# VectorE sums the halves of a value product before it takes a gate reciprocal

## The reference

```
s = einsum('bqkgd,bskd->bkgqs', qb, k) * scale ; p = softmax(s)
ob = einsum('bkgqs,bskd->bqkgd', p, v)
o  = concat(rms_norm(oa) * (1 - lam_init) * silu(ga), ob * silu(gb))
x  = x + gate * (o @ w_out)
```

## Time and profile before

| | |
|---|---|
| median of 3 runs | 1225.95 us (1225.51 to 1226.72) |
| profiled execution, its own time | 1226.55 us |
| its span, first to last instruction | 1224.7 us |
| TensorE busy | 1188.2 us, 97% |
| VectorE busy | 838.8 us, 68% |
| ScalarE busy | 587.2 us, 48% |
| GpSimd busy | 255.0 us, 21% |
| mean granted TensorE clock | 0.998 |

### The profile page before, as it was taken

The page is one execution under the profiler, slowest core; times in us unless marked ns, Lnnn a source line. Parts: engine busy times, 40 slices in busy tenths (PEclk is TensorE's granted clock), DMA queues, the critical chain, the costliest instruction groups (busy, mean ns, idle before and its releaser), DMA issues. The chain is left out here.

```text
span 1224.7 us, 16455 instructions
## 1 busy us (share of the span) xinstructions
PE 1188.2 (97%) x5915; PEld 958.7 (78%) x5915; DVE 838.8 (68%) x1266; ACT 587.2 (48%) x1240; POOL 255.0 (21%) x439
## 2 busy tenths in 40 slices
PE   5899999999999999999999999999999999999996
PEld 3455788788887888888888888888878888788885
DVE  4445488877778777767767675767757574879764
ACT  5522324546455464545646455556556655212223
POOL 1211032012030120222222322222233322210111
PEclk9999999999999999999999999999999999999999
DMA  9999242735537366363544545353544412956644
GB/s 352 370 378 378 88 113 78 206 94 173 159 104 202 94 178 167 92 170 93 140 142 121 144 119 143 105 160 90 150 148 118 130 57 76 316 166 224 190 143 176
DMA packets 169777, 200.47 MB, mean 164 GB/s; under 512 B 11760, under 2 KB 129168, under 8 KB 168928
## 3 DMA queue, kind: packets, MB, share of 16 engines
q1 hardware_dynamic: 155824, 153.65, 41.0%
q0 software_dynamic: 13424, 45.20, 11.5%
q10 hardware_dynamic: 448, 0.57, 0.1%
HBM read 166.20 MB, written 33.18 MB: 163 GB/s over the span
## 5 line engine op out<-in xcount | busy, mean ns | idle before, releaser
L806 PE MATMUL z_ps<-w_hi,xt_hi 128*128 128x512 f32 x1350 | 543.7, 403 | 2.7 <-issue 1.1
L808 PE MATMUL z_ps<-w_hi,xt_lo 128*128 128x512 f32 x1350 | 526.9, 390 | 0.0
L807 PE MATMUL z_ps<-w_lo,xt_hi 128*128 128x512 f32 x1350 | 526.5, 390 | 0.0
L1113 ACT ACTIVATE w_hi<-w_raw 128x512 fp32r<-128x512 f32 x270 | 169.3, 628 | 384.2 <-PE z_ps L808 260.9
L806 PEld LDWEIGHTS z_ps<-w_hi,xt_hi 128*128 128x128 f32 x1350 | 253.9, 188 | 72.4 <-issue 27.2
L808 PEld LDWEIGHTS z_ps<-w_hi,xt_lo 128*128 128x128 f32 x1350 | 253.4, 188 | 54.6
L1575 DVE TENSOR_TENSOR w_lo<-w_raw,w_hi 128x512 fp32r<-128x512 f32 x270 | 193.0, 718 | 149.7 <-ACT w_hi L1113 149.1
L807 PEld LDWEIGHTS z_ps<-w_lo,xt_hi 128*128 128x128 f32 x1350 | 254.3, 188 | 43.3
L2059 POOL TENSOR_TENSOR sg<-sg,zs 128x128 f32<-128x128 f32 (+1 forms) x60 | 42.8, 713 | 406.5 <-DVE sg L1645 406.3
L1676 DVE TENSOR_REDUCE small<-s_sb 128x2 f32<-128x1536 f32 (+1 forms) x60 | 87.7, 1462 | 40.1 <-ACT s_sb L1113 40.1
L1276 ACT ACTIVATE s_sb<-s_sb,small 128x768 f32<-128x768 f32 (+1 forms) x120 | 98.1, 821 | 9.7 <-DVE small L1676 9.6
(11 more groups left out here) (203 smaller groups left out, 1317.9 us busy)
## 6 DMA issues: line engine op xcount, KB each, us to landing
w_raw<-in_w_in_dram SPq DMA_DIRECT2D x188, 256.0 KB, 3.4
ada_raw<-in_w_ada_dram SPq DMA_DIRECT2D x64, 512.0 KB, 11.6
p_spill<-s_sb SPq DMA_DIRECT2D x56, 384.0 KB, 2.8
w_raw<-in_w_out_dram SPq DMA_DIRECT2D x64, 256.0 KB, 4.0
p_pair<-p_spill SPq DMA_DIRECT2D x64, 192.0 KB, 3.9
gate_raw<-in_w_ada_dram POOLq DMA_DIRECT2D x12, 1024.0 KB, 8.2
p_block<-p_spill SPq DMA_DIRECT2D x96, 96.0 KB, 2.4
w_raw<-in_w_in_dram POOLq DMA_DIRECT2D x20, 256.0 KB, 6.3
```

What stands on the lines that cost most here:

```text
L806: pe.matmul(out, hi_l, hi_r, start=start, stop=False)
L807: pe.matmul(out, hi_l, lo_r, start=False, stop=False)
L808: return pe.matmul(out, lo_l, hi_r, start=False, stop=stop)
L1113: return act.activation(out, in_, ACT.Copy, **kw)
```

## The change

In a step in which a value product and a gate reciprocal both stand, VectorE now adds the halves first. The list `early_values` holds the V entries of such a step; they are done ahead of `gate_inverse` and left out of the later loop. Such steps are 7, 9 and 11, and `o_high` has work in them while the four pairs of G heads are attended to. For D heads the same code runs and issues nothing.

```diff
--- before.py
+++ after.py
@@ -1934,14 +1934,20 @@
                         norm_reduce(it - 1)
                     if c_step == 2:
                         v_lo(it - 1)
+                    early_values = [(a, t) for kind, a, t in late if kind == "V"] if s in gate_at(it) else []
+                    for a, t in early_values:
+                        if not v_first(late):
+                            o_high(a, t)
                     if s in gate_at(it) and group_kind(it - 1) != "KV":
                         gate_inverse(it - 1, gate_at(it)[s])
+                else:
+                    early_values = []
                 for kind, a, t in late:
                     if kind == "QK":
                         qk_los(a)
                     elif kind == "S":
                         score_max(a, t)
-                    elif kind == "V" and not v_first(late):
+                    elif kind == "V" and not v_first(late) and (a, t) not in early_values:
                         o_high(a, t)
                     elif kind == "GT":
                         gated_turned(a, t)
```

## The result

The changed kernel takes 1231.39 us (median of 6 runs, 1231.01 to 1232.47) against 1226.4 for the kernel before (also the median of 6 runs): 5.0 us or 0.4% slower, ratio 1.004 with a 95% interval of 1.003 to 1.005. The prediction was 5.1 us slower and 1231.0. Its profiled execution has a span of 1229.5 us (before 1224.7), a granted TensorE clock of 0.998 as before, and the same 16455 instructions.

What follows compares the result with a forecast made beforehand. TensorE, busy 1188.2 of 1224.7 us, was taken to bound the kernel. Steps 7, 9 and 11 summed to -0.12+0.2+1.19 = +1.27 us per item, times 4 +5.1, giving a median of 1231.0 us (1229.5 to 1232.3).

Steps and rivals of the forecast that it cites:

- The bank wait goes: Step 7: TensorE's second score piece no longer waits for the sum; 0.49 of 0.75 us kept at the third piece.
- The gain is lost again before tile 1's value product: Step 8: later transposes hold the row maximum, so only 0.12 us per item of step 7's 0.49 stays.
- no contention: Rival 1: GpSimd's multiply yields to w_lo, 1227.2 us, no measurable change; chance 0.14 together with rival 4, no effect.
- The multiply meets w_lo: After each swapped reciprocal, GpSimd's gate multiply lengthens VectorE's w_lo, the weight's low part, by 0.41 us per swap.
- Step 9's cover is just used up: Step 9: a delay of 1.94 us meets 1.75 of cover before the row maximum; loss 0.2 us per item.
- Step 11 has no cover of that kind: Step 11: the same 1.94 us, without idle time before the low parts, delays tile 3's value product; loss 1.19 per item.
- the slow restart: Step 11's term for TensorE after its stall at tile 3's value product: 0.08 us per item.
- The cover of 0.83: Slack of VectorE's low parts before TensorE reaches tile 3's value product: 0.83 us.
- Nothing catches up behind it: After step 11, TensorE's later queue is late too, and ScalarE and VectorE follow it, so the loss stays.
- The full block: Rival 2: w_lo fully blocked by the multiply, or p_pair late for tile 4; 1232.7 to 1233.5 us, chance 0.14.
- The faster one: Rival 3: the whole 0.75 us per item stays and step 11's lateness misses TensorE; 1222.9 us, chance 0.05.
- The change that does nothing: Rival 4: the sum waits for ScalarE anyway; within rival 1's time of 1227.2 us, chance 0.14 together with rival 1.

Runs made afterwards that it cites:

- the single swaps: Three kernels with the swap in step 7, 9 or 11 alone, the other steps as before: 1226.09, 1227.59 and 1231.34 us against 1226.61 for the kernel before.
- the kernel with the gated row first: Kernel before, but in step 7 VectorE takes the sum and the gated row ahead of the gate reciprocal: 1226.98 against 1226.59 us.
- with the multiply held: Changed kernel, but GpSimd's gate multiply of steps 7, 9 and 11 waits until the next step's w_lo is done: 1227.54 us against 1226.61 for the kernel before.

## Why the prediction was right

Each step of the sum against what the changed kernel and the single swaps show, per item:

- **The bank wait goes** (step 7). Right: the second score piece starts without a gap, and the third is the one that waits, for the gated row, 0.37 after its forerunner instead of 0.23. I had put that wait at 0.21; it is 0.14.
- **The gain is lost again before tile 1's value product.** Predicted -0.12, measured -0.15. With the meeting taken away it is -0.48, which is the 0.49 that the step gave for no contention.
- **The multiply meets w_lo.** Predicted +0.41, measured 1.16-0.69 = +0.47. The rule read from two rows (what the multiply has to go, less 0.14) held: 0.61 to go gives 0.47, in all 12 meetings within 0.02. The size was off because the gated row behind the reciprocal is 0.06 shorter than the one I took, so w_lo starts sooner into the multiply. The forecast did not suffer: by this rule the end of w_lo hangs on the multiply's end and not on its own start, so the two sizes offset each other and the delay stayed at 1.94.
- The Trainium skill's rule ("SBUF — State Buffer", "Who interferes with whom"), by which the second comer is fully blocked, would have given 0.61 here; the chip shows 0.47 of it, and in the kernel with the gated row first 0.53 of 0.66. The contention and its side (the first comer goes on undisturbed) are as that page says. In the price the measured rows decide: 0.14 less. Whether the two really overlap for that time, or the second is only shown as started before it is stopped, no run here tells.
- **Step 9's cover is just used up.** Predicted +0.2, measured +0.22 in the changed kernel and +0.23 alone; with the multiply held, where the delay is 1.94-0.47 = 1.47 and lies under 1.75, it is +0.03.
- **Step 11 has no cover of that kind.** Predicted +1.19, measured +1.12 at tile 3 and +0.07 at tile 4, where the slow restart that I had put in step 11 shows up: the matmul behind the stalled one follows after 0.31 instead of 0.23. The cover of 0.83 was confirmed from both sides, by 1.95 and 1.47 (late) and 0.7 (not late).
- **Nothing catches up behind it.** Right: 5.04 in the stretch of the G items and 5.0 in the medians. The span is 4.8 longer, as the changed trace came 0.18 ahead into that stretch. That the medians meet the forecast to 0.1 us is in part chance, with an interval of 3.7 to 6.1 us; the agreement of the starts, step by step, is not. SyncE's later p_pair cost nothing: the value products of tile 4 are late by no more than the restart.
- The rivals: no contention (1.2 us slower) is what the held kernel gives, 0.9 us slower, but not this one. The full block needed 0.55 or more on w_lo and a loss of 6.7 us; w_lo has 0.47, the loss is 5.0, and no p_pair was late. The faster one falls at its own condition: the low parts had 0.83 of slack and needed 1.95. The change that does nothing falls with step 7, whose sum now starts at 218.92.

## What to carry to other kernels

Where an instruction waits for another engine's result, what stands ahead of it is free as long as it fits the wait. Moving it behind makes the whole of it late, so a swap pays only where the waited-for operand is already there. Price it place by place: three swaps alike in code were worth -0.15, +0.23 and +1.19 us per item here, and what decided was each place's slack before the next thing TensorE needs. Look also at what the moved instruction triggers on an engine that it can collide with: the multiply that follows the reciprocal was worth 4.1 of the 5.0 us. And if a long instruction stands in the way, look for idle time in an earlier step before changing its order in the same one: that was worth 3.3 us where the swap lost 5.0.

## What the runs showed of the hardware

Two of VectorE's instructions with two SBUF operands, w_lo and the gate scale, and GpSimd's multiply, which also has two, stop one another, and the second to start loses. Behind a running multiply, VectorE's instruction took longer by what the multiply had to go less 0.14 us, in five sizes: 0.15 to go gave 0.02, 0.29 gave 0.14, 0.41 gave 0.26, 0.61 gave 0.47 and 0.66 gave 0.53. The other way round the same sum holds: when w_lo was first by 0.16 us it was not slowed and had 0.47 to go, and the multiply took 1.05 instead of 0.73 us; when the gate scale was first, with 0.26 to go, it took 0.85. The gated row, with one operand in SBUF and one in PSUM, started 0.49 before the multiply's end and took 0.42, the same as with no multiply beside it.

That the loser of one meeting then holds up VectorE's next instruction I had not expected: being first in a pair of instructions is no protection for the one behind.

TensorE restarts slowly after a stall: the matmul behind the first one follows after 0.31 instead of 0.23 us, at all 12 stalls of the changed kernel (0.30 or 0.31).
